# MLP units regrouped in a decoder layer: both up units of a chunk, then both down units

## The reference

```python
def channel_mlp(x, g, w_up, w_down):
    h = rmsnorm(x, g)
    u = jnp.maximum(jnp.einsum('btd,df->btf', h, w_up), 0)
    return jnp.einsum('btf,fd->btd', u * u, w_down)
```

## Time and profile before

| | |
|---|---|
| time, median of 3 runs (lowest to highest) | 2329.32 us (2328.99 to 2330.38) |
| profiled execution, its own time | 2329.08 us |
| its span | 2327.3 us |
| TensorE busy | 2275.8 us, 98% of the span |
| VectorE busy | 1673.3 us, 72% |
| ScalarE busy | 1167.4 us, 50% |
| granted TensorE clock, mean | 0.993 of full speed |

### The profile page before, as it was taken

How to read it: one execution, slowest core, us unless ns; L and a number is a source line. 1 busy time by engine, 2 the same in 40 slices (tenths; PEclk the granted TensorE clock), 3 DMA queues, 4 the chain that set the end, 5 groups by cost and what they waited for, 6 DMA issues and landing times.

```text
span 2327.3 us, 37075 instructions
## 1 busy us (share of the span) xinstructions
PE 2275.8 (98%) x14142; PEld 2002.6 (86%) x14142; DVE 1673.3 (72%) x3613; ACT 1167.4 (50%) x2366; POOL 94.1 (4%) x161
## 2 busy tenths in 40 slices
PE   9999999999999999999999999999999999999998
PEld 8877899888887898898998788899888778989886
DVE  4588877777378877777457887777756788777775
ACT  4565554445375644445355564454535646444433
POOL 2000000000000000000000210000110000000000
PEclk9999999999999999999999999999999999999999
DMA  6212333324511233234521232333444112322222
GB/s 198 82 46 81 100 100 109 95 96 157 165 57 55 74 108 97 95 107 140 159 82 37 69 98 95 100 100 109 154 123 136 47 53 80 100 82 89 85 82 77
DMA packets 176652, 227.92 MB, mean 98 GB/s; under 512 B 15507, under 2 KB 126708, under 8 KB 176460
## 3 DMA queue, kind: packets, MB, share of 16 engines
q1 hardware_dynamic: 162636, 192.63, 26.5%
q10 hardware_dynamic: 6448, 19.40, 2.3%
q0 software_dynamic: 7392, 13.52, 2.1%
HBM read 214.13 MB, written 12.60 MB: 97 GB/s over the span
## 4 chain that ended last, share of the span: by engine, by line
PE 86%; DVE 8%; ACT 4%; issue 1%; DMA 0%; ACTq 0%; DVEq 0%
PE ps L2486 18%; PE ps L2488 17%; PE ps L2487 17%; PE ps L3000 8%; PE ps L3001 8%; PE ps L2999 8%; PE ps L2497 2%; DVE a_lo L1477 1%; ACT wide L878 1%; DVE wide L1911 1%; DVE w_lo L1438 1%; PE ps L2620 1%; PE ps L2611 1%; ACT wide L1110 1%; PE ps L2680 1%
## 5 line engine op out<-in xcount | busy, mean ns | idle before, releaser
L2486 PE MATMUL ps<-w_hi,u_all 128*128 128x512 f32 x1024 | 403.1, 394 | 1.5 <-DVE w_lo L1438 1.5
L2488 PE MATMUL ps<-w_hi,u_all 128*128 128x512 f32 x1024 | 404.2, 395 | 0.0
L2487 PE MATMUL ps<-w_lo,u_all 128*128 128x512 f32 x1024 | 400.2, 391 | 0.0
L875 ACT ACTIVATE w_hi<-PT 128x512 fp32r<-128x512 f32 x224 | 128.9, 622 | 340.5 <-PE ps L2488 236.9
L1477 DVE TENSOR_TENSOR x<-x,ps 128x512 f32<-128x512 f32 (+1 forms) x288 | 196.5, 685 | 135.8 <-PE ps L2488 118.1
L2486 PE MATMUL ps<-w_hi,a_hi 128*128 128x290 f32 (+1 forms) x768 | 264.6, 345 | 9.3 <-DVE om L2046 6.4
L3000 PE MATMUL ps<-a_lo,w_hi 128*128 128x256 f32 (+1 forms) x896 | 255.8, 285 | 0.0
L3001 PE MATMUL ps<-a_hi,w_lo 128*128 128x256 f32 (+1 forms) x896 | 255.2, 285 | 0.0
L2999 PE MATMUL ps<-a_hi,w_hi 128*128 128x256 f32 (+1 forms) x896 | 255.2, 285 | 0.0
L2487 PE MATMUL ps<-w_lo,a_hi 128*128 128x290 f32 (+1 forms) x768 | 254.7, 332 | 0.0
L2488 PE MATMUL ps<-w_hi,a_lo 128*128 128x290 f32 (+1 forms) x768 | 254.4, 331 | 0.0
(11 more groups left out here) (426 smaller groups left out, 4957.4 us busy)
## 6 DMA issues: line engine op xcount, KB each, us to landing
w_raw<-in_w_up_dram SPq DMA_DIRECT2D x128, 512.0 KB, 3.9
w_raw<-in_w_down_dram SPq DMA_DIRECT2D x128, 512.0 KB, 3.5
w_raw<-in_w_out_dram SPq DMA_DIRECT2D x32, 512.0 KB, 3.5
w_raw<-in_w_in_dram SPq DMA_DIRECT2D x24, 580.0 KB, 4.7
w_raw<-in_w_in_dram SPq DMA_DIRECT2D x22, 512.0 KB, 3.7
w_raw<-in_w_in_dram SPq DMA_DIRECT2D x32, 256.0 KB, 3.0
x<-in_x_prompt_dram ACTq DMA_DIRECT2D x9, 512.0 KB, 6.0
bias<-bias_rows POOLq DMA_DIRECT2D x32, 128.0 KB, 3.4
```

Of the source, the lines that this page charges most:

```text
L875: eng.activation(form_at(w_hi_all, u, f), form_src(q, u, name), ACT.Copy).then_inc(f_high.sem, 1)
L2486: eng.matmul(out, lh, rh, start=(k == ks[0]), stop=False)
L2487: eng.matmul(out, lh, rl, start=False, stop=False)
L2488: ins = eng.matmul(out, ll, rh, start=False, stop=(k == last))
```

## The change

`MLP_ORDER` alone is changed. In chunks 1 to 6 the order U(c,0) D(c-1,0) U(c,1) D(c-1,1) becomes U(c,0) U(c,1) D(c-1,0) D(c-1,1). Chunk 7 keeps the alternating order, and D(7,0) D(7,1) follow as before.

```diff
 MLP_ORDER = [("U", 0, 0), ("U", 0, 1)]
 for _c in range(1, NC):
-    MLP_ORDER += [(kind, _c - (kind == "D"), half) for half in range(2) for kind in "UD"]
+    if _c < NC - 1:
+        MLP_ORDER += [(kind, _c - (kind == "D"), half) for kind in "UD" for half in range(2)]
+    else:
+        MLP_ORDER += [(kind, _c - (kind == "D"), half) for half in range(2) for kind in "UD"]
 MLP_ORDER += [("D", NC - 1, 0), ("D", NC - 1, 1)]
```

## The result

| | before | after |
|---|---|---|
| median of 4 runs, us | 2329.85 (2328.99 to 2330.93) | 2345.85 (2344.76 to 2350.33) |
| profiled execution, its own time | 2329.08 | 2346.88 |
| its span | 2327.3 | 2345.1 |

A forecast was written before the change was run, and what follows sets the result against it. TensorE, busy for all of the MLP window, was taken to bound the kernel. Added stalls of 9.6 + 0.6 + 0.45 + 1.6 = 12.3 us on 2329.08 gave 2341.4, with 0.24 for the median 2341.6 us; range 2337 to 2347.

The forecast's parts named there:

- Term 1: Product 5 of U(1,0): TensorE waits for a VectorE addition that stands behind four sums; stall 1.28 us.
- Terms 1 to 3: Chunk 1: stalls of 1.28, 0.57 at products 5, 6 of U(1,0), 1.35 at product 5 of U(1,1); 3.20 per quarter.
- Term 4: Chunks 2 to 6, product 5 of U(c,1): stall 0.04, 15 times, plus 0.15 three times for chunk 2's ring wrap.
- Term 5: Last quarter's chunk 1: four stalls of 0.13, 0.7, 0.55 and 0.25 us, together 1.6.
- What hides the rest: MLP: loads have 2 us of cover, ring slots come 7 us ahead, down units have over 1 us of VectorE cover.
- the lower bound: Whole kernel: no restart cost beyond 0.05 and every chain met 0.1 sooner leaves a loss of 9 us.
- rivals 1 and 2: The first: the clock falls after the new stalls, 2345 us, chance 0.12; the second: late seams, 2346, chance 0.08.
- Rival 2: Seams of chunks 2 to 6: 0.3 us of contention in each of 15 makes 4.5, 2346 us; chance 0.08.
- Rival 3: VectorE's back-to-back steps cost full length, each of 18 seams 1.2 us later: +21, 2363 us; chance 0.01.
- Rival 4: Product 5: the additions are not late, only terms of tenths remain, say 2332 us; chance 0.05.
- Rival 5: Faster: the second of two adjacent down units runs closer to its weight loads, up to 2.07 us per pair; chance 0.01.

The follow-up runs named there:

- the fourth run: The whole change, with VectorE's first three additions in U(1,0) ahead of the second pair of sums and the low parts; 16.5 us above the kernel before, ratio 1.0068.
- The fifth run: The whole change, with the order of waits turned round in front of two VectorE instructions; 13.0 us above the kernel before, ratio 1.0054.

## Why the prediction was right

- **The bound.** "The change cannot win time by removing a wait there; the question is whether it adds one" held. The new waits are of the one kind named, products 5 and 6 on additions.
- **Term 1** (1.28): the first addition of U(1,0) ran 7.82 us into the unit (258.55 in the trace after, the unit starting at 250.73), exactly as laid out. TensorE resumed 1.17 late, and its second matmul 0.11 later still: 1.28.
- **Terms 1 to 3** together, 3.20 per quarter: 3.26 measured. Whether they are three prices is another matter: the fourth run shows that taking terms 1 and 2 away alone wins nothing. Summing them was right only because each stall was worked out with the earlier ones already in.
- **Term 4 was mis-sized**, and it makes the difference between 12.3 and 16: "Stall 0.04, 15 times", plus 0.15 for each wrap, 1.05 in all. Measured were 0.34 and 0.48, some 5.5 in the trace and 5.1 by the run of chunks 2 to 6 alone. The step that failed first is the start "sums at 2.14": they started at 2.35 (341.10 - 338.75), because the first sum waits for the last low part (0.12 more, it stood in the listing of the new order as a wait for `f_split`), and because several waits cost 0.1 before that sum. The step "addition 16.57" took 0.1 too little once more, for the same reason. Those 0.3 us fell on a chain with no room left, so they counted in full, 15 times. The fifth run took the two tenths of the waits away and left the rest.
- **Term 5** (1.6): 1.50 over the last quarter's MLP, 1.70 in its chunk 1. The starts of its matmuls show all four small stalls; two are long enough to stand in the list of waits.
- **What hides the rest** held: no wait for loads, none for weights that was not there before, down pairs 22.20.
- **The range** began at 2337, though the lower bound of 9 us gives 2338.3. The measured 2345.85 lies near its upper end, and the range reached that far because of rivals 1 and 2.
- **The rivals.** The clock did not fall: each of the windows above shows a granted clock of 1.00, the full 2.4 GHz, also where the stalls are. Rival 2, late seams, is what happened in place and size (0.34 a seam, 0.3 foreseen; its 2346 is nearer to the 2345.85 measured than the forecast is, and it had a chance of 0.08). The cause is another: a wait that was left out and two wait instructions, and not contention. Rival 3 is out: two sums still take 1.29 where one takes 0.69. The Trainium skill (VectorE: DVE Perf Modes, The DRAIN you can't avoid) has the next operation wait until the pipe is empty, but adds in the same place that one which is not held starts earlier; the prediction left that half out. By the first half two sums would take 1.38 or more, an estimate from twice 0.69; the 1.29 agrees with the second half. Rival 4 is out by the trace. Rival 5 is out: a down pair takes 22.20, two single down units 22.16. Something was won by the new order, but in the seven units (below).

## What to carry to other kernels

Before two like units are put side by side, write out what each engine does between the events that the bound engine waits for, with every wait for an own result and every instruction with more than one wait counted; a chain that comes out within 0.1 us of its due time should be priced as late. A stall taken away at the front of such a chain is worth nothing unless the chain behind it is shortened too: here two lines moved on ScalarE were worth 12 us, and the earlier additions on VectorE nothing until those two had been moved, and then another 4.

## What was not expected of the hardware

- An instruction with three or four waits has them spread over a separate wait instruction (0.05 us in the records) and itself. If the wait that is met last is in the separate one, the step costs 0.82 us where 0.72 is usual; written first, it rides on the instruction and the 0.1 is gone. Turning two such orders round took 3.3 us out of the MLP in the traces of this kernel (3.0 by the medians). The wait instruction ahead of the first sum (count; shortest, median and longest in ns):

```profile
L1465 DVEq EVENT_SEMAPHORE  x52: 49/50/50, 255.0 to 2271.4; - x52
```

- Two seven units side by side without a stall take 19.84 us, two single ones 19.96. The change between matmuls of 256 and of 512 columns isn't the cause: in the trace after, U(7,0) has down units on both sides and takes 9.92 as well. The difference lies in product 2 alone, 1.36 us there and 1.42 in the kernel before. Why these 12 matmuls follow each other faster when the unit before was another seven unit, or the second of two down units, stays open. It is far below the 0.51 per pair that rival 5 needed. The windows are product 2 before, then U(7,0) and its product 2 after:

```profile
884.64:886.06 1.42, 1.42 (x14) 1.42 (x13) 1.27 (x2) 1.18 (x2) 0.00 (x0) 1.00 0.54 120
```

```profile
508.68:518.60 9.92, 9.92 (x86) 9.92 (x85) 6.61 (x11) 5.21 (x8) 0.00 (x0) 1.00 0.44 124
511.53:512.89 1.36, 1.36 (x15) 1.36 (x13) 1.22 (x2) 1.18 (x2) 0.00 (x0) 1.00 0.57 120
```
